# Forget-gate weights in one load, row norms split in halves, and three engines on the last output columns

## What is computed

```
h    = rms_norm(x, g_pre)
proj = h @ w_in      # q_a k_a v_a gate_a (512 columns each), f_a (8), q_b k_b v_b gate_b (512 each)
F    = cumsum(log_sigmoid(f_a + forget_b))
y_a  = softmax(q_a k_a / 8 + F[t] - F[s], causal) v_a * silu(gate_a)
y_b  = softmax(q_b k_b / 8 - slope * (t - s), causal) v_b * silu(gate_b)
y    = concat(y_a, y_b) @ w_out
out  = x + rms_norm(y, g_post)
```

## Time and profile before

| | |
|---|---|
| median of 3 runs | 153.03 us (152.94 to 153.65) |
| the profiled execution's own time | 154.46 us |
| its span, first to last instruction | 152.5 us |
| busy in the span: TensorE, VectorE, ScalarE, GpSimd | 93%, 74%, 63%, 32% |
| mean granted TensorE clock | 0.977 |

### The profile page before, as it was taken

One profiled execution on the slowest core, in us unless ns is written; L12 is line 12 of the kernel. 1 busy time (PEld: TensorE's weight loads), 2 busy tenths in 40 slices (PEclk: granted clock), 3 DMA queues, 4 the chain that ended last, 5 costly groups with the idle time before them and its releaser, 6 DMA issues.

```text
span 152.5 us, 2938 instructions
## 1 busy us (share of the span) xinstructions
PE 142.0 (93%) x1020; PEld 133.6 (88%) x1020; DVE 112.8 (74%) x241; ACT 96.8 (63%) x199; POOL 48.1 (32%) x67
## 2 busy tenths in 40 slices
PE   7993999999999999999899999999999999999940
PEld 7992899999999989998899999999999888898840
DVE  0644918799999898856979897998979797220493
ACT  5455786717991799489487778686776855215430
POOL 7500000000000000708329393919375574201230
PEclk9999599999999999999999999999999999999995
DMA  3889995497789779880846463636451180000034
GB/s 106 233 255 390 392 373 181 148 349 254 241 258 315 260 299 413 314 267 9 221 156 192 140 198 132 210 140 209 138 171 35 49 295 0 0 4 0 0 116 160
DMA packets 14524, 29.05 MB, mean 191 GB/s; under 512 B 2472, under 2 KB 7088, under 8 KB 14128
## 3 DMA queue, kind: packets, MB, share of 16 engines
q1 hardware_dynamic: 14064, 27.57, 53.7%
q10 hardware_dynamic: 448, 1.32, 2.2%
HBM read 25.73 MB, written 1.06 MB: 176 GB/s over the span
## 4 chain that ended last, share of the span: by engine, by line
PE 64%; DVE 20%; DMA 5%; ACT 4%; SPq 3%; issue 1%; DVEq 0%; ACTq 0%
PE bank L801 26%; PE bank L960 15%; DVE w_lo L549 9%; PE bank L811 9%; PE bank L913 6%; DMA raw<-in_w_f 5%; ACT w_hi L369 3%; DVE wo_lo L630 2%; DVE h L594 2%; PE bank L894 2%; PE bank L896 2%; PE bank L895 2%; SPq L202 2%; DVE gate L638 2%; DVE v L607 1%
## 5 line engine op out<-in xcount | busy, mean ns | idle before, releaser
L549 DVE TENSOR_TENSOR w_lo<-raw,w_hi 128x1024 fp32r<-128x1024 f32 (+1 forms) x34 | 47.1, 1386 | 8.0 <-ACT w_hi L369 7.6
L369 ACT ACTIVATE w_hi<-raw 128x1024 fp32r<-128x1024 f32 (+1 forms) x34 | 35.8, 1059 | 6.2 <-DVE logits L645 3.6
L801 PE MATMUL bank<-h_hi,w_hi 128*128 128x256 f32 x128 | 35.8, 280 | 0.4 <-DVE h_lo L650 0.4
L801 PE MATMUL bank<-h_lo,w_hi 128*128 128x256 f32 x128 | 35.7, 279 | 0.0
L801 PE MATMUL bank<-h_hi,w_lo 128*128 128x256 f32 x128 | 35.7, 279 | 0.0
L306 POOL TENSOR_TENSOR bias<-squares,causal 128x256 f32<-128x256 f32 (+1 forms) x8 | 12.0, 1525 | 55.0 <-DMA squares<-decay_rows_scratch 55.0
L801 PEld LDWEIGHTS bank<-h_hi,w_hi 128*128 128x128 f32 x128 | 24.1, 188 | 1.1 <-DVE h_lo L650 0.6
L801 PEld LDWEIGHTS bank<-h_lo,w_hi 128*128 128x128 f32 x128 | 24.0, 188 | 0.5
L801 PEld LDWEIGHTS bank<-h_hi,w_lo 128*128 128x128 f32 x128 | 24.0, 188 | 0.0
L323 POOL TENSOR_TENSOR probs<-probs,row_inv 128x256 f32<-128x256 f32 (+1 forms) x16 | 12.9, 828 | 29.4 <-DVE row_inv L681 29.4
L464 ACT ACTIVATE probs<-logits,neg_max 128x128 f32<-128x128 f32 (+1 forms) x32 | 14.2, 445 | 7.8 <-DVE neg_max L675 7.8
(11 more groups left out here) (118 smaller groups left out, 308.7 us busy)
## 6 DMA issues: line engine op xcount, KB each, us to landing
raw<-in_w_units SPq DMA_DIRECT2D x30, 512.0 KB, 4.1
raw_out<-in_w_out SPq DMA_DIRECT2D x4, 512.0 KB, 4.6
v_pair<-v SPq DMA_DIRECT2D x8, 256.0 KB, 3.9
raw<-in_w_out SPq DMA_DIRECT2D x4, 512.0 KB, 3.4
h<-in_x SPq DMA_DIRECT2D x1, 1024.0 KB, 9.0
squares<-decay_rows_scratch ACTq DMA_DIRECT2D x1, 1024.0 KB, 8.0
x_t<-in_x SPq DMA_DIRECT2D x1, 1024.0 KB, 5.0
raw<-in_w_units SPq DMA_DIRECT2D x3, 256.0 KB, 4.3
```

The lines of the kernel that those rows point to most:

```text
L369: nc.scalar.activation(w[0][:, s, 0:width], raw[:, s, 0:width], ACT.Copy).then_inc(s_hi, 1)
L549: nc.vector.tensor_tensor(w[1][:, s, 0:width], raw[:, s, 0:width], w[0][:, s, 0:width].bitcast(F32), ALU.subtract).then_inc(s_lo, 1)
L801: last = nc.tensor.matmul(dst, stationary(a, j), moving(b, j), start=n == 1, stop=n == count * len(PASSES))
```

## The change

- One load of all forget weights (`wf`, 32 KB) on ScalarE's queue takes the place of the eight on SP's. GpSimd copies the 8 columns of each unit into their place in `raw` (`forget_columns`), the first four before it makes the masks, the others behind them and behind the low part of the unit four before. `unit_high` waits for that copy (`s_wf`).
- x for units 2 and 3 comes in two loads and not in one; x for units 4 and 5 and for 6 and 7 goes behind units 3 and 4 in the queue.
- x in rows comes in two halves, issued right behind the loads of units 5 and 6. ScalarE squares them behind the high parts of units 5 and 6. The load of f_bias goes behind unit 7.
- VectorE makes the low part of unit 6 ahead of the norms and that of unit 7 right behind the diagonals, ahead of the copy of `rrow`. TensorE spreads the norms behind unit 6.
- Nine warm-up products and not twelve.
- Tail: `times_g` of group 3 leaves its product in PSUM; VectorE makes the residual of groups 2 and 3. Group 4 is scaled by ScalarE and added by GpSimd, and SP issues its 256 columns.

```diff
-X_LOADS = ((0, 1), (1, 2), (2, 4), (4, 6), (6, 8))
-WARM_UP = 12
+X_LOADS = ((0, 1), (1, 2), (2, 3), (3, 4), (4, 6), (6, 8))
+WARM_UP = 9
...
+        wf = sb("wf", [P, KT, HEADS])
...
-            def load_forget(u):
-                sp.dma_start(raw[:, u % RING, D_MODEL:V_WIDTH], w_f[:, u, :]).then_inc(s_f_in[u % RING], 16)
-
             load_x(0)
             load_values(0, 0, SEQ, s_piece_in[0])
             load_values(0, SEQ, HALF, s_piece_in[1])
             load_values(0, HALF, D_MODEL, s_raw_in[0])
-            load_forget(0)
             load_x(1)
             load_values(1, 0, HALF, s_piece_in[2])
             load_values(1, HALF, D_MODEL, s_raw_in[1])
-            load_forget(1)
             for u in range(PIECED, RING):
                 load_x(u)
                 load_values(u, 0, D_MODEL, s_raw_in[u])
-                load_forget(u)
-            load_x(RING)
...
             for u in range(RING, V_UNITS):
+                if u < len(X_LOADS):
+                    load_x(u)
+                else:
+                    t = u - len(X_LOADS)
+                    sp.dma_start(x_rows[:, t, :], x[:, t, :]).then_inc(s_xrows_in[t], 16)
                 sp.wait_ge(s_lo, u + 1 - RING)
                 load_values(u, 0, D_MODEL, s_raw_in[u % RING])
-                load_forget(u)
-                if u == RING:
-                    sp.dma_start(x_rows, x).then_inc(s_xrows_in, 16)
-                    sp.dma_start(fb_row[:, :], f_bias.rearrange("h o -> o h").to_broadcast((P, HEADS))).then_inc(s_fb_in, 16)
+            sp.dma_start(fb_row[:, :], f_bias.rearrange("h o -> o h").to_broadcast((P, HEADS))).then_inc(s_fb_in, 16)
...
+            sp.wait_ge(s_last, 1)
+            sp.dma_start(out[1, :, HALF + SEQ:], x_nat[:, 1, HALF + SEQ:]).then_inc(s_stored, 16)
...
+            def forget_columns(u):
+
+                if u >= RING:
+                    pool.wait_ge(s_lo, u + 1 - RING)
+                pool.tensor_copy(raw[:, u % RING, D_MODEL:V_WIDTH], wf[:, u, :]).then_inc(s_wf, 1)
...
+            pool.wait_ge(s_wf_in, 16)
+            for u in range(RING):
+                forget_columns(u)
             pool.memset(causal[:, :], 0.0).then_inc(s_pool, 1)
...
+            for u in range(RING, V_UNITS):
+                forget_columns(u)
...
+            pool.wait_ge(s_yscaled_last, 1)
+            pool.tensor_tensor(x_nat[:, 1, HALF + SEQ:], x_nat[:, 1, HALF + SEQ:], y_post[:, 1, HALF + SEQ:],
+                               ALU.add).then_inc(s_last, 1)
...
                 if width == V_WIDTH:
-                    act.wait_ge(s_f_in[s], n)
+                    act.wait_ge(s_wf, (n // 16 - 1) * RING + s + 1)
...
             act.dma_start(gpre_col[:, :], g_pre).then_inc(s_g_in, 16)
+            act.dma_start(wf[:, :, :], w_f).then_inc(s_wf_in, 16)
...
-            unit_high(0, 32, 1, V_WIDTH)
-            act.wait_ge(s_xrows_in, 16)
+                else:
+                    unit_high(c % RING, 32, c + 1 - RING, V_WIDTH)
+            act.wait_ge(s_xrows_in[0], 16)
             row_squares(0)
+            unit_high(2, 32, 3, V_WIDTH)
+            act.wait_ge(s_xrows_in[1], 16)
             row_squares(1)
-            unit_high(1, 32, 2, V_WIDTH)
             act.wait_ge(s_ms, 1)
             act.wait_ge(s_table, 1)
             nc.scalar.activation(root[:, :], ms[:, :], ACT.Sqrt).then_inc(s_root, 1)
-            unit_high(2, 32, 3, V_WIDTH)
...
-            act.wait_ge(s_fin[TT - 1][1], 1)
-            act.dma_start(out[TT - 1, :, HALF:], x_nat[:, TT - 1, HALF:]).then_inc(s_stored, 16)
+            act.wait_ge(s_ypost, len(out_groups))
+            act.wait_ge(s_rstd, TT + 1)
+            nc.scalar.activation(y_post[:, 1, HALF + SEQ:], y_post[:, 1, HALF + SEQ:], ACT.Copy,
+                                 scale=rstd[:, 1:2]).then_inc(s_yscaled_last, 1)
+            act.wait_ge(s_fin[1][1], 1)
+            act.dma_start(out[1, :, HALF:HALF + SEQ], x_nat[:, 1, HALF:HALF + SEQ]).then_inc(s_stored, 16)
...
-                elif c < RING:
-                    unit_low(c, c + 1, V_WIDTH)
-            unit_low(0, 5, V_WIDTH)
-            unit_low(1, 6, V_WIDTH)
+                else:
+                    unit_low(c % RING, c + 1, V_WIDTH)
+            unit_low(2, 7, V_WIDTH)
...
-            unit_low(2, 7, V_WIDTH)
+            unit_low(3, 8, V_WIDTH)
             dve.wait_ge(s_rbc, 1)
             nc.vector.tensor_copy(rrow[:, :], rrow_ps[:, 0:SEQ]).then_inc(s_rrow, 1)
-            unit_low(3, 8, V_WIDTH)
...
-                nc.vector.tensor_tensor(y_post[:, t, cols], group, gpost_row[:, cols], ALU.mult).then_inc(s_ypost, 1)
+                kept = group if n == 3 else y_post[:, t, cols]
+                nc.vector.tensor_tensor(kept, group, gpost_row[:, cols], ALU.mult).then_inc(s_ypost, 1)
...
-                cols = slice(c * HALF, (c + 1) * HALF)
-                nc.vector.scalar_tensor_tensor(out=x_nat[:, t, cols], in0=y_post[:, t, cols], scalar=rstd[:, t:t + 1],
+                cols = out_groups[groups - 1][1]
+                kept = out_groups[3][2] if groups == 4 else y_post[:, t, cols]
+                nc.vector.scalar_tensor_tensor(out=x_nat[:, t, cols], in0=kept, scalar=rstd[:, t:t + 1],
...
-            residual(1, 1, 5)
+            residual(1, 1, 4)
...
-            for u in range(PIECED, 6):
+            for u in range(PIECED, 7):
                 value_unit(u)
...
             last.then_inc(s_rbc, 1)
-            for u in range(6, V_UNITS):
-                value_unit(u)
+            value_unit(7)
```

More of the change, by code:

```diff
@@ L77, in hybrid_layer @@
         gpost_row = sb("gpost_row", [P, D_MODEL])
-        row_ssq = sb("row_ssq", [P, 72])
+        wf = sb("wf", [P, KT, HEADS])
+        row_ssq = sb("row_ssq", [P, HEADS])
         raw = sb("raw", [P, RING, V_PITCH])
@@ L149, in hybrid_layer @@
         s_piece_in = [sem(f"first_piece_{c}_in") for c in range(3)]
-        s_f_in = [sem(f"w_f_in{s}") for s in range(RING)]
+        s_wf_in, s_wf = sem("w_f_in"), sem("forget_columns")
         s_raw_out_in = [sem(f"raw_out_in{s}") for s in range(2)]
@@ L160, in hybrid_layer @@
         s_table = sem("activation_table")
-        s_xrows_in, s_ssq = sem("x_rows_in"), sem("row_squares")
+        s_xrows_in, s_ssq = [sem(f"x_rows_in{t}") for t in range(TT)], sem("row_squares")
         s_ms, s_root, s_rstd = sem("mean_square"), sem("root_ready"), sem("rstd_ready")
@@ L184, in hybrid_layer @@
         s_fin = [[sem(f"fin_ready{t}{c}") for c in range(2)] for t in range(TT)]
+        s_yscaled_last, s_last = sem("last_columns_scaled"), sem("fin_last_columns")
         s_stored = sem("stored")
@@ L265, in _ @@
                              x_nat[:, t, c * HALF:(c + 1) * HALF]).then_inc(s_stored, 16)
-            sp.wait_ge(s_stored, 16 * 2 * TT)
+            sp.wait_ge(s_last, 1)
+            sp.dma_start(out[1, :, HALF + SEQ:], x_nat[:, 1, HALF + SEQ:]).then_inc(s_stored, 16)
+            sp.wait_ge(s_stored, 16 * (2 * TT + 1))
         @block.gpsimd
@@ L397, in _ @@
                         if last:
-                            act.wait_ge(s_f_in[c], 16)
+                            act.wait_ge(s_wf, c + 1)
                         nc.scalar.activation(w[0][:, c, lo:hi], raw[:, c, lo:hi],
```

## The result

The changed kernel takes 152.25 us in the median of 12 executions (151.70 to 152.83), the kernel before 153.47 in the median of 12 on the same chip (152.67 to 154.95). The ratio is 0.9919 with a 95% interval of 0.9896 to 0.9941: 0.8% faster, 1.2 us. The forecast was 153.2 us against 153.03, 0.2 us slower, with a range of 151.6 to 154.3. The time lies in the range, but the kernel became clearly faster where no measurable change was forecast. The profiled execution took 152.47 us, its span is 150.7.

The account below looks back on a forecast made before the run. Loads bound TensorE's start, VectorE the stretch from rrow to the query products, TensorE the rest. Query products +0.39 and tail -0.2 gave +0.2 us: 153.2 against 153.03 us, range 151.6 to 154.3.

Parts of the forecast that it names:

- start of unit 2: TensorE's first product of unit 2 was to come 1.3 us earlier, at 13.1, with bounds of 0.3 and 2.5 us.
- the tail: Last residuals split over VectorE, ScalarE and GpSimd: 0.2 us gained; bounds 0.25 us gained and 0.5 us lost.
- One more unit ahead of rrow: TensorE makes rrow after unit 6, not 5: 2.83 us more, less 1.14 for VectorE's low part of unit 7.
- The prediction's own signs: Wrong if VectorE has gaps in the gate stage, unit 2 starts before 12.1, or the granted clock stays full.
- The norms are no nearer bound: Diagonals of the row norms ready at about 25 us, while TensorE ends unit 6 at about 29.
- Rival 2: The clock doesn't fall after TensorE's idle time before unit 2; rrow comes 1.7 us sooner: 151.5 us, chance 0.14.
- The forget weights: Three small loads leave the path to unit 2 (0.5 us), one of 32 KB comes (0.17): net 0.33 us earlier.
- the slow stretch: Loads at 138 GB/s from 7.5 to 9.0 us, thought nearer to the queue's start-up; 0.35 us gain taken, up to 1.9 possible.
- Rival 1: The small loads held up the queue; unit 2 starts up to 2.5 us earlier: 152.0 us, chance 0.14.
- The warm-up and the pieces: Warm-up ends at 4.80 instead of 6.07, units 0 and 1 start about 1 us earlier; worth nothing by itself.
- rrow and the VectorE stretch: From rrow's copy to TensorE's first query product the chain lies almost wholly on VectorE, 27.95 to 56.35 us before.
- The hidden things: GpSimd's eight copies, its later constants, ScalarE's extra issue and the reordered loads were to cost nothing, being covered.

## Why the prediction was wrong

The terms of the sum beside the two profiles of before, in us (the first is the one the sum was made on; "without" is the other one):

| term | forecast | before with the fall | before without |
|---|---|---|---|
| start of unit 2 | -1.3 | -2.01 | -1.39 |
| from there to rrow's copy | +2.83 | +1.26 | +2.29 |
| from there to the query products | -1.14 | -1.01 | -1.48 |
| so the query products | +0.39 | -1.76 | -0.58 |
| from there to the last rstd | 0 | -0.31 | -0.26 |
| the tail | -0.2 | +0.26 | +0.24 |
| so the span | +0.2 | -1.81 | -0.60 |

**One more unit ahead of rrow: the step that failed.** The sum charged 2.83 us for it and took 1.14 back for the low part of unit 7, 1.69 us in all. It measured 0.25 us against the profile with the fall and 0.81 against the one without.

Against the first the reason is the clock. I carried one fall over to the changed kernel, 1.7 us in rrow. With 0.32 us of idle time there was none ahead of rrow. The copy of rrow came at 27.20 instead of 29.5: 0.7 from the earlier start, 1.6 from the clock. The second profile of the changed kernel has none either; its 21 other executions have mean clocks of 0.986 to 0.997, by which a fall can't be ruled out in the lowest of them. In the 14 profiles the clock fell behind 2.64 and 2.24 us of idle TensorE, and not behind 1.86, 1.36 or less. The prediction's own signs said so: wrong if the granted clock stays full.

Against the second the reason is what bounds rrow in before. Without a fall TensorE is early, and the norms set rrow, at 26.30; so the added unit costs 0.54 us less. And VectorE no longer waits 0.38 us for ScalarE's high part of unit 7. "The norms are no nearer bound" was true only while the clock fell.

I made the sum on an execution that wasn't typical. Its own time stood 1.43 us over the median; I subtracted that as a constant, where it held a fall that at least two thirds of the executions of before don't have. Rival 2 had the event, but priced it (151.5) against a kernel before that always falls. By the medians of before a fall costs 0.7 us there, not 1.7, because the norms hide the rest; where TensorE sets rrow, in the run with the norms alone, it costs 1.6. The pair without a fall gives 0.6 us of span, 0.8 of own time (153.31 to 152.47); the medians are 1.2 apart. What is left of that isn't taken apart.

**The start of unit 2: about right in size, wrong in its parts.** I had 1.3 us; it was 2.0 and 1.4. The forget weights had 0.33 of it, and 0.35 for the slow stretch; alone they brought 1.1 to 1.7 us. I leaned to the start of the queue as the cause of the slow stretch, because small loads also stand in a fast one. It needed the small loads and the one load of x for two units. The price of a small load is not the 0.17 us by which it lands behind its unit, but what later loads lose, and it has no one size. For each of the three ahead of unit 2 it is 0.4 to 0.6 us in the run with the forget weights alone, 0.2 to 0.3 with the small loads put back (13.01 against 12.35 and 12.24), and under 0.1 for the additional ones of 4 KB (12.51). The Trainium skill's 0.68 us for 4 KB ("DMA: Bandwidth & Descriptors", Bandwidth), which it gives for transfers that GpSimd issues, is above all of these. Rival 1 had the mechanism, the small loads, and its 152.0 lies 0.25 us from the result; but its way there, unit 2 up to 2.5 us earlier with one fall, is not what happened. That its number came so near is in part luck.

**The warm-up and the pieces: wrong.** Units 0 and 1 were to start 1 us earlier. They started at 5.55 and not at 5.83, for the first piece landed at 5.0 and not at 3.7, beside the new load on ScalarE's queue. With the small loads back, and that load gone, they start at 4.85, the forecast's 1 us. The late pieces, the early unit 2 and TensorE's waits for pieces between 5 and 8 us closed the idle time that I had put at 2.2 to 2.7 us. The 18 warm-up instructions themselves took 3.69, 3.72, 3.88 and 4.21 us in four of the runs. In the fastest they start 0.21 us apart up to about 4 us and 0.11 us from there on, in the slowest 0.21 us apart throughout. This agrees with the Trainium skill ("TensorE: Matmul & The Clock Gate", Part 1), by which the moment of a clock change differs from run to run.

**rrow and the VectorE stretch: right.** The rule by which the sum was made holds in all 14 profiles: the query products start 27.4 to 27.5 us behind rrow's copy when the low part of unit 7 is done ahead of it (27.20 to 54.59; with the norms alone moved 30.20 to 57.59), and 28.4 us behind it when that part comes after it (24.72 to 53.13 with rrow behind unit 5). Where VectorE also waits 0.38 us for ScalarE it is 28.9 (26.30 to 55.17). The new order of the norms costs 0.7 us by itself where there is no fall, 1.1 by all medians. Behind the faster loads it wasn't measured alone: the whole change is as fast as the forget weights alone, but it also holds the new x loads and the tail.

**The tail: the wrong sign.** 0.2 us to be gained; 0.24 lost. The engines did as forecast: GpSimd's add took 0.73 us, at the low end of 0.65 to 1.40, and the residual from PSUM beside it 0.48 us. That agrees, as far as it goes, with the Trainium skill ("GPSIMD Engine Reference", Specifications), which names VectorE instructions with two SBUF inputs as those that contend; no run has this residual without the add beside it. But the last issue came only 0.05 us sooner behind rstd, and it landed in 2.3 us, not in 2.0, though it carries half the bytes. I had taken the landing as the same. Why it is longer, with two other outputs issued in the 0.6 us before it, was not tested.

**The hidden things** stayed hidden: GpSimd's copies took 0.19 to 0.45 us each, and nobody waited for them or for the masks.

## What to carry to other kernels

A small load in a queue that feeds the whole kernel should be priced by what all later loads lose, not by its own landing: eight loads of 4 KB cost 0.9 us here with nobody using their data, and by the trace most of it passed through one later load, x in rows, on which rrow hung. Before a sum is made on a profiled execution, ask whether it is a typical one; its distance from the median may hold an event, here a fall of the clock, that the change removes or that most executions never had. A fall priced where TensorE is the bound (1.6 us) is not its price where another engine is (0.7 us). And a part that takes an engine's idle time away is worth nothing where another order bounds the end: the norms' new order removed 3.3 us of VectorE's idle time, and cost 0.7 to 1.1 us by itself.

## What the hardware showed beyond that

- Eight loads of 128 rows cost 0.9 us with rows of 32 bytes and 1.4 us with rows of 256 bytes. SP's issue of each takes some 0.45 us, and in both unit 2's load is issued 0.95 us later than in the changed kernel (5.44 against 4.49). Unit 2 started only 0.2 to 0.3 us later with the 32 bytes and 0.7 to 0.8 with the 256 (13.04), so the issue alone isn't the price. What in the queue is, wasn't separated.
- With one load of 32 KB on ScalarE's queue, issued at 1.18 us beside SP's first two pieces of 128 KB, 17 of 18 such pieces landed 3.2 to 3.9 us behind their issue and one 2.7 (nine profiles); without it 2.4 to 2.9 us (five profiles, the changed kernel with the small loads back among them).
- The last output, 128 KB, landed in 2.3 us where the last one of 256 KB had taken 2.0.
- With ten filler products none of 12 executions had a fall of the clock, and the kernel was not faster for it (ratio 1.0032, 0.9997 to 1.0066).
